# Recurrent chunks' inversion: products of the first five levels as 32x32 tiles on the array's diagonal

## The reference, cut to what matters

```python
def rwkv7_step(state, inp):
    r_t, w_t, k_t, v_t, kk_t, a_t = inp
    sa = jnp.einsum('bhvk,bhk->bhv', state, -kk_t)
    state = (state * w_t[:, :, None, :] + sa[..., None] * (kk_t * a_t)[:, :, None, :]
             + v_t[..., None] * k_t[:, :, None, :])
    y = jnp.einsum('bhvk,bhk->bhv', state, r_t)
    return state, y
...
    _, y = lax.scan(rwkv7_step, s0, (tm(rh), tm(wh), tm(kh), tm(vh), tm(kk), tm(ah)))
```

## Time and profile before

| | |
|---|---|
| median of 3 runs | 2630.66 us (2630.11 to 2630.99) |
| the profiled execution | 2630.19 us, its span 2628.2 us |
| granted TensorE clock, mean | 0.997 |
| busy: PE, PEld, DVE, ACT, POOL | 98%, 79%, 59%, 42%, 16% of the span |
| recurrent phase | from 2257 to 2509 us |

### The profile page before, as it was taken

How to read it: one execution, slowest core, us unless ns; L and a number is a source line. 1 busy time by engine, 2 the same in 40 slices (tenths; PEclk the granted TensorE clock), 3 DMA queues, 4 the chain that set the end, 5 groups by cost and what they waited for, 6 DMA issues and landing times.

```text
span 2628.2 us, 46698 instructions
## 1 busy us (share of the span) xinstructions
PE 2567.8 (98%) x19224; PEld 2086.1 (79%) x19224; DVE 1561.6 (59%) x2521; ACT 1108.6 (42%) x2067; POOL 425.6 (16%) x381
## 2 busy tenths in 40 slices
PE   8999999999999999999999999999999999999998
PEld 6887777778778998899888777766776677788876
DVE  8765443436686665676546676355567646656754
ACT  3242233323355543556335554324445545344521
POOL 4421221100000000000000000111112100456644
PEclk9999999999999999999999999999999999999999
DMA  6753443134423454534534222631011253100032
GB/s 227 212 119 107 97 131 101 65 115 165 160 102 116 144 192 141 189 132 150 170 127 173 76 96 90 270 129 49 29 49 49 85 189 105 42 19 19 19 129 96
DMA packets 80754, 307.24 MB, mean 117 GB/s; under 512 B 7200, under 2 KB 8864, under 8 KB 62624
## 3 DMA queue, kind: packets, MB, share of 16 engines
q1 hardware_dynamic: 55984, 238.72, 25.9%
q0 software_dynamic: 12800, 33.56, 5.6%
q10 hardware_dynamic: 11760, 31.99, 3.2%
HBM read 268.32 MB, written 69.47 MB: 129 GB/s over the span
## 4 chain that ended last, share of the span: by engine, by line
PE 83%; DVE 9%; ACT 4%; issue 3%; DMA 1%; POOL 1%; DVEq 0%; ACTq 0%; SPq 0%; POOLq 0%
PE ps L425 46%; PE ps L3270 4%; PE ps L1258 4%; PE ps L1257 4%; PE ps L1259 4%; PE ps L2145 2%; PE ps L2191 2%; PE ps L2171 2%; PE ps L2072 2%; PE ps L609 2%; PE ps L635 1%; PE ps L2074 1%; PE ps L2073 1%; PE ps L624 1%; DVE parts L404 1%
## 5 line engine op out<-in xcount | busy, mean ns | idle before, releaser
L425 PE MATMUL ps<-parts,parts 128*128 128x512 f32 (+2 forms) x6456 | 1467.5, 387 | 15.9 <-DVE parts L804 8.8
L425 PEld LDWEIGHTS ps<-parts,parts 128*128 128x128 f32 x6456 | 1171.6, 188 | 299.7 <-issue 34.3
L404 DVE TENSOR_TENSOR parts<-ring,parts 128x1024 fp32r<-128x1024 f32 x180 | 220.8, 1238 | 174.7 <-ACT parts L381 166.3
L381 ACT CAST parts<-ring 128x1024 fp32r<-128x1024 f32 x183 | 188.7, 1044 | 116.9 <-DMA ring<-in_weights 62.1
L1257 PE MATMUL ps<-parts,parts 128*128 128x256 f32 x840 | 236.2, 281 | 1.3 <-ACT phase_data L1406 1.3
L1258 PE MATMUL ps<-parts,parts 128*128 128x256 f32 x840 | 236.1, 281 | 0.0
L1259 PE MATMUL ps<-parts,parts 128*128 128x256 f32 x840 | 236.0, 281 | 0.0
L404 POOL TENSOR_TENSOR parts<-ring,parts 128x1024 fp32r<-128x1024 f32 x62 | 153.2, 2472 | 423.1 <-DVE parts L381 423.0
L2552 POOL TENSOR_TENSOR phase_data<-phase_data,stream 128x512 f32<-128x512 f32 x12 | 17.2, 1436 | 1186.2 <-PE ps L2082 1186.2
L867 DVE TENSOR_TENSOR_SCAN stream<-stream 128x513 f32<-128x513 f32 (+3 forms) x96 | 95.2, 992 | 173.2 <-ACT stream L737 173.0
L1257 PEld LDWEIGHTS ps<-parts,parts 128*128 128x128 f32 x840 | 158.7, 189 | 2.4 <-ACT phase_data L1406 1.5
(11 more groups left out here) (391 smaller groups left out, 3761.6 us busy)
## 6 DMA issues: line engine op xcount, KB each, us to landing
ring<-in_weights SPq DMA_DIRECT2D x128, 1024.0 KB, 4.9
up_sums<-in_weights POOLq DMA_DIRECT2D x24, 1024.0 KB, 8.9
ring<-in_weights SPq DMA_DIRECT2D x32, 512.0 KB, 4.3
ring<-up_sums SPq DMA_DIRECT2D x30, 512.0 KB, 5.9
phase_data<-up_sums SPq DMA_DIRECT2D x60, 256.0 KB, 5.6
up_sums<-up_sums POOLq DMA_DIRECT2D x8, 1024.0 KB, 5.4
phase_data<-in_weights SPq DMA_DIRECT2D x30, 256.0 KB, 5.5
raw_keep<-phase_scratch SPq DMA_DIRECT2D x21, 256.0 KB, 2.4
```

The lines of the kernel that those rows point to most:

```text
L381: cast(self.hi(p), self.whole(p)).then_inc(self.k.hi_ready, 1)
L404: g.tensor_tensor(self.lo(p), self.whole(p), self.hi(p).bitcast(F32), ALU.subtract).then_inc(self.k.lo_ready, 1)
L425: last = pe.matmul(out, a, b, start=i == 0 and a is ah and b is bh, stop=i == len(pairs) - 1 and a is al)
```

## The change

`group_blocks` is added: the same product as eight 32x32 matmuls, for each of the two slots one on each of the four 32x32 tiles of the array's diagonal (rows and columns 0 to 31, 32 to 63, 64 to 95, 96 to 127). `group_of` picks it for levels 0 to 4 of chunks 1 to 15. Chunk 0 and the last level keep `group_pairs`. What lies outside the diagonal 32x32 blocks is no longer written in PSUM at these levels; it keeps the zeros that chunk 0 left there. So that the last level does not overwrite them, its X and its W go to columns of their own in the same banks (`x_at`, `w_at`), and the copy and the add read there. The copies (128x128) and the adds (128x128) are as large as before.

```diff
+    def x_at(l):
+
+        return 2 * CHUNK if l == LEVELS - 1 else 0
+
+    def w_at(l):
+
+        return 4 * CHUNK if l == LEVELS - 1 else 2 * CHUNK
...
+        def group_blocks(i, bank, at, lhs, rhs):
+
+            out = k.bank(bank)[:, at:at + 2 * CHUNK].rearrange("p (m c) -> p m c", m=2)
+            for m in range(2):
+                for q in range(4):
+                    here, side = slice(32 * q, 32 * q + 32), slice(32 * (q % 2), 32 * (q % 2) + 32)
+                    last = pe.matmul(out[here, m, side], lhs(2 * i + m, here, side), rhs(2 * i + m, here, side),
+                                     start=True, stop=True)
             return last
+
+        def group_of(c, l):
+
+            return group_blocks if c and l < LEVELS - 1 else group_pairs
...
         def inv_w(c, l):
 
+            multiply = group_of(c, l)
             for i in range(2):
                 pe.wait_ge(x_ready[i], (LEVELS - 1) * c + l)
                 pe.wait_ge(g_ready[i], LEVELS * c + l)
                 if l < LEVELS - 1:
-                    group_pairs(i, w_bank[i], 0, lambda m, e: gg[rows(e), c % 2, m],
-                                lambda m, e: xx[rows(e), l % 2, m])
-                group_pairs(i, w_bank[i], 2 * CHUNK, lambda m, e: xx[rows(e), l % 2, m],
-                            lambda m, e: gg[rows(e), c % 2, m]).then_inc(w_mm[i], 1)
+                    multiply(i, w_bank[i], 0, lambda m, r, s: gg[r, c % 2, m, s], lambda m, r, s: xx[r, l % 2, m, s])
+                multiply(i, w_bank[i], w_at(l), lambda m, r, s: xx[r, l % 2, m, s],
+                         lambda m, r, s: gg[r, c % 2, m, s]).then_inc(w_mm[i], 1)
```

More of the change, by code:

```diff
@@ L3269, in group_pairs @@
                 for e in range(2):
-                    last = pe.matmul(out[rows(e), m], lhs(2 * i + m, e), rhs(2 * i + m, e), start=True, stop=True)
-            return last
+                    last = pe.matmul(out[rows(e), m], lhs(2 * i + m, rows(e), slice(0, CHUNK)),
+                                     rhs(2 * i + m, rows(e), slice(0, CHUNK)), start=True, stop=True)
+            return last
+        def group_blocks(i, bank, at, lhs, rhs):
[5 more added lines that the diff above has]
+                                     start=True, stop=True)
+            return last
+        def group_of(c, l):
+            return group_blocks if c and l < LEVELS - 1 else group_pairs
         def raw(c):
@@ L3298, in inv_x @@
             pe.wait_ge(off_ready, LEVELS * c + l + 1)
+            multiply = group_of(c, l)
             for i in range(2):
                 if l == 0:
-                    last = group_pairs(i, x_bank[i], 0, lambda m, e: off[rows(e), c % 2, 0, m],
-                                       lambda m, e: eye[rows(e)])
+                    last = multiply(i, x_bank[i], 0, lambda m, r, s: off[r, c % 2, 0, m, s], lambda m, r, s: eye[r, s])
                 else:
                     pe.wait_ge(t_ready[i], (LEVELS - 1) * c + l)
-                    last = group_pairs(i, x_bank[i], 0, lambda m, e: off[rows(e), c % 2, l, m],
-                                       lambda m, e: tt[rows(e), 0, m])
+                    last = multiply(i, x_bank[i], x_at(l), lambda m, r, s: off[r, c % 2, l, m, s],
+                                    lambda m, r, s: tt[r, 0, m, s])
                 last.then_inc(x_mm[i], 1)
         def inv_w(c, l):
+            multiply = group_of(c, l)
             for i in range(2):
@@ L3478, in _ @@
                             a.wait_ge(w_mm[i], n - 2)
-                        a.copy(xx[:, l % 2, G[i]], half(x_bank[i], 0)).then_inc(x_ready[i], 1)
+                        a.copy(xx[:, l % 2, G[i]], half(x_bank[i], x_at(l))).then_inc(x_ready[i], 1)
                     if l == 2 and c == 0:
@@ L3619, in _ @@
                         v.wait_ge(g_ready[i], LEVELS * c + l)
-                        v.tensor_tensor(gg[:, c % 2, G[i]], gg[:, c % 2, G[i]], half(w_bank[i], 2 * CHUNK),
+                        v.tensor_tensor(gg[:, c % 2, G[i]], gg[:, c % 2, G[i]], half(w_bank[i], w_at(l)),
                                         ALU.add).then_inc(g_ready[i], 1)
```

## The result

| | before | with the change |
|---|---|---|
| median | 2630.39 us (2629.71 to 2630.99, 4 runs) | 2671.00 us (2669.30 to 2671.84, 4 runs) |
| the profiled execution | 2630.19 us, span 2628.2 | 2670.34 us, span 2668.3 |
| mean granted clock | 0.997 | 0.985 |

The ratio is 1.0153, with a 95% interval of 1.0137 to 1.0169: the change costs 40.6 us. The prediction said 2616 us, a gain of 14.5, and its range ended at 2635; a slower kernel had a chance of 0.15 there.

A forecast was written before the change was run, and what follows sets the result against it. The recurrent phase was taken as a relay between engines; 8 x 0.77 + 3 x 1.5 + 2 x 1.3 + 2 x 0.6 = 14.5 us off 2630.19, median 0.5 above, gave 2616 us, range 2609 to 2635.

The forecast's parts named there:

- The price of a product: Group products on TensorE: four turns of four tiles at 0.033 us each, 0.13 us in place of 0.234.
- record price: Rival for W and X of levels 0 to 4: a group product takes 0.47 us; 2695 us, chance 0.10.
- two abreast: Rival: only two tiles work at a time, a group product takes 0.26 us; 2636 us, chance 0.05.
- floor: Rival: a turn is no shorter than 0.0585 us, products stay 0.234, switches cost; 2635 us, chance 0.12.
- The change of shape: On TensorE, going from 64x64 to 32x32 tiles or back costs 0.15 us.
- T0 at +0.51: In a plain chunk, VectorE's first add starts 0.51 us behind W, in place of 0.73.
- The legs: Five stretches of a plain chunk, W1 to the next W1: 0.77 us saved in all, 15.16 to 14.39.
- GpSimd in time: In plain chunks GpSimd, busy 8.0 of 15.16 us, was taken to have `off` ready in time.
- The legs with the change: Step summing savings between W products: 0.77 us a plain chunk, more in long ones, 14.5 us in total.
- the price is the record, not the tile: Rival: TensorE starts pairs no faster than one per 0.029 us; about 4.2 us a chunk lost, 2695 us, chance 0.10.
- I charge nothing for the clock: Recurrent chunks: longest new TensorE idle stretch below 1 us, under `chunk_masked`, so no cost for a lower clock.
- The long chunks: Chunks 9 to 11: W3 and W4 save 0.42 us each, 1.5 us a chunk; chunks 8 and 12 save 1.3.

The follow-up runs named there:

- e12: The changed kernel with two of the four tiles, each matmul issued twice, half of the inversion left out: 2680.86 us, ratio 1.0208.
- e5: The changed kernel with two of the four tiles (half of the inversion left out) and two unread filler products a chunk: 2623.26 us, ratio 0.9974.
- e9: The changed kernel with 32x32 tiles only for W of level 3 (chunks 1 to 15) and level 4 (chunks 8 to 12): 2627.28 us, ratio 0.9992.
- e8: The whole changed kernel plus two unread filler products a chunk: 2672.49 us, ratio 1.0158.
- e3: The changed kernel with each 32x32 matmul issued twice: 2853.54 us, ratio 1.0853.
- e1: The changed kernel with only two of the four tiles of each product, half of the inversion left out: 2627.44 us, ratio 0.9993.
- e10: The changed kernel with 32x32 tiles only for W of levels 3 and 4 in chunks 8 to 12: 2626.56 us, ratio 0.9988.
- e7: The changed kernel with 32x32 tiles only for W of levels 2 and 3 in chunks 1 to 15: 2629.62 us, ratio 0.9996.

## Why the prediction was wrong, and where it was right

**The steps that held.** *The price of a product.* The prediction took four tiles at once and 0.033 us a turn, 0.13 us for a product. In the timeline of the change the products of W2 start at 2296.00, 2296.12 and 2296.24: 0.12. Two tiles alone take 0.25 (e12), so the third and fourth work beside them. So the three rivals that priced the tile (record price, two abreast, floor) are out as prices of a product. *The change of shape*, 0.15 us: 23 pairs from 2297.89 to 2298.21 are 0.17 at the pace of 0.0075 and 0.15 more; 5 pairs from 2294.12 to 2294.30 leave 0.14. *T0 at +0.51*, here W1 of chunk 6:

```profile
2367.02 0.22 PEld L3288 LDWEIGHTS ps<-phase_data,stream 32*32 32x32 f32 x16 [0.45 <-ACT phase_data L3502]
...
2367.55 0.29 DVE L3640 TENSOR_TENSOR stream<-stream,ps 128x128 f32<-128x128 f32 x1 [0.37 <-PE ps L3288]
```

0.53, in place of 0.73 in the earlier trace rows. *The legs*: 14.3 us a plain chunk where the clock was full and the instructions were as many as before (e5), 0.24 for W3 alone (e9). *Copies and adds* keep their lengths: L3640 takes 0.29 as L3617 did. *GpSimd in time*: TensorE waited 2.3 us for L3038 in the phase, before 3.0.

**The step that failed** is "The legs with the change". It let TensorE go from one record pair to the next as fast as the array takes them and asked only what engine is waited for. Each leg is shorter by what the array saves, and longer by what the instruction stream needs: 416 instructions more a chunk are 1.6 blocks, 6.1 us of stream at 3.74, of which a chunk had 4.4 to spare (15.16 less 10.8). The chunk of 14.39 us that was forecast would have had 3.6. The sum needed one line for it: 1154 / 256 x 3.74 = 16.9 us, more than 14.39, so the stream bounds the chunk. The expectations of the runs counted some 12 to 16 instructions a chunk more than there are (1170 and 750), which changes none of their readings. Nothing in the trace of before gives this price. The 10.5 us of "issue" that L3270's weight loads have there are not its sign: five stops of 0.76 us stand right behind a 128x512 matmul of L3188, while PE is at work, and the longest, 1.5 us, ends with an add of L3617 by the matmul row.

The rival "the price is the record, not the tile" (chance 0.10) had the direction right and came nearest of the four in time (2695). Half of it is borne out: over a long run TensorE gets a *pair* every 2 x 0.0146 = 0.029 us, the very pace it had in the two-tile stretches of before. The other half is refuted: it put that price on every product, 0.47 us, and a product takes 0.12, its pairs 0.0075 us apart; what is slow is the block, once every 256 instructions. So it charged 4.2 us a chunk where the stream alone costs 1.7 (e8). The time worked out with the Trainium skill's 25 ns between small matmuls (TensorE: Matmul & The Clock Gate, Back-to-back issue gap), some 2675 us, is nearer still, by luck: the traces don't agree with that figure between different tiles, where pairs start 0.0075 us apart. Another page of the Trainium skill bears on what did happen (Runtime: NRT & Kernel Launch, Instruction fetch mechanics): each engine is fed in blocks of 16 KiB, 256 instructions, the next one fetched while the current one runs, and crossing a boundary is "mostly hidden". The traces agree on the block's size, by the 16 KB packets and the 256 from stop to stop, and not on the hiding: a boundary was an idle 0.8 to 0.9 us in chunk 2 of the change and 1.7 to 1.9 in e3.

**"I charge nothing for the clock"** failed too. e1 has no more instructions than before and the clock was low for 54 us all the same: in this kernel shorter products were enough for it. The text looked at the longest new idle stretch ("below 1 us") and took that for the answer. What the clock costs there can be put at 11 us (2627.4 less the 2616 that its legs give), and e5 gets 4 of them back. How much of the change's 40.6 us is the clock stays open. At e1's price, 11 us for 54 low, its 63 us would be 13, but that price leans on the forecast's 2616. Between the runs of e1 itself, 2619.5 us at a mean clock of 0.990 and 2635.0 at 0.983, 37 us of low clock go with 15.5 us, and at that price it would be 26. From the other side: a plain chunk at full clock loses 1.7 us (e8) and chunks 9, 10 and 11, at PEclk 1.00 in the change, lose 0.4, 2.7 and 0.4, so that the stream alone comes to some 17 us, and to 24 if the other four chunks lose 1.7 too. All of these are estimates. e8 took away 10 us of low clock and won nothing. The stream and the clock are not independent either: a stop is idle time of PE, ahead of a fall.

The long chunks were a term that held in part. With W3 and W4 alone (e10) the prediction's 0.42 each make 0.84 us a chunk. Cut at `turn`, chunks 9, 10 and 11 take 16.99, 17.36 and 17.37 us in e10, and 17.78, 17.78 and 18.16 before: gains of 0.79, 0.42 and 0.79. What holds back chunk 10 was not followed up.

## What to carry to other kernels

Before splitting a matmul into smaller tiles, count the instructions of the stretch, not only the array's time: an fp32 matmul is four, and here TensorE got 256 in 3.7 us over a longer stretch, so over a longer stretch nothing is gained from pairs of records that the array could start less than 0.03 us apart, however many tiles run side by side. "Issue" in front of TensorE's matmuls in the middle of a group that waits for nothing, at every 256th instruction, is the sign of it. And a TensorE that finishes sooner may fall to its lower clock, so the stretch should be priced at both levels.

## What the runs showed of the hardware that was not expected

- Sustained supply of TensorE: 256 instructions in 3.7 us. The transfer is not what takes that long. The DMA view of the change from 2288 to 2326 us (packets, MB, share of 16 engines):

```profile
q8 instruction: 9, 0.15, 1.7%
```

  9 blocks in 38 us, and 1.7% of 16 x 38 us is 10.3 us, 1.15 us of transfer for each. What fills the other 2.6 us was not tried. Single restarts with 252 matmul instructions between them stand 3.5 to 5.8 us apart in the changed kernel, so 3.7 is a pace over a longer stretch.
- The longest stop of the change, 3.02 us, stands where the DMA engines were busiest; its rows are a window and the weight loads at its end:

```profile
2350.40:2357.20 6.80, 3.50 (x188) 2.89 (x181) 2.40 (x10) 0.81 (x3) 0.00 (x0) 1.00 0.46 157
```

```profile
2356.09 0.20 PEld L3288 LDWEIGHTS ps<-stream,phase_data 32*32 32x32 f32 x11 [3.02 <-issue]
```

  The load of 1 MB from `gate_keep` runs there, and the chunk (5) takes 20.6 us. The same load ends just ahead of the stop of 1.58 us in chunk 5 of e9 (17.64 us), and that chunk of e7, with a stop of 2.2 us, takes 17.75; before, the chunk takes 15.16 us with the load in it. That a block comes later when it queues behind other traffic fits all of this, but no run moved the load away to test it.
- Four diagonal 32x32 tiles took 16 fp32 pairs of 32 columns in 0.12 us, 0.0075 each, and two of them took 0.25: the third and the fourth tile work beside the other two.
- The clock fell with the same number of matmuls when they were smaller (e1), though PE was still marked busy for 226.7 of 252 us from 2257 on, before for 239.6. Before it fell in chunk 1 of the change PE had been busy 5.12 of 6.80 us, in the rows shown above.
